# Mixture-of-experts stage: 32-row blocks on four column tiles instead of pairs of 64-row blocks, in a two-layer trunk

## The reference

```
def grouped_expert_mlp(h, expert_id, w_gate, w_up, w_down):
    '''Evaluate only the selected experts: assignments are sorted by expert into EXPERT_BLOCK-row
    segments (each padded to a block multiple) and every block is run through its own expert.
    h: (N, D); expert_id: (N, K) -> (N, K, D).'''
```

```
layer 0:  73 30 51 12 71 45 82 44 128 231 49 145 174 205 146 334 22 102 84 18 109 52 44 43 39 15 25 36 49 56 7 39
layer 1:  42 21 14 87 41 178 91 12 65 55 16 57 37 2 70 4 9 25 6 23 10 2 12 25 177 156 10 66 6 5 548 176
```

## Time and profile before

| | |
|---|---|
| median of 3 runs | 5775.29 us |
| profiled execution | 5788.05 us, of which span 5785.7 us |
| TensorE (PE) busy | 4182.2 us, 72% |
| VectorE (DVE) busy | 2196.7 us, 38% |
| ScalarE (ACT) busy | 1422.0 us, 25% |
| DMA moved | 778.83 MB, mean 135 GB/s |
| weights of the experts | 3 x 64 transfers of 2048 KB |

### The profile page before, as it was taken

How to read it: one execution, slowest core, us unless ns; L and a number is a source line. 1 busy time by engine, 2 the same in 40 slices (tenths; PEclk the granted TensorE clock), 3 DMA queues, 4 the chain that set the end, 5 groups by cost and what they waited for, 6 DMA issues and landing times. The chain is left out here.

```text
span 5785.7 us, 71070 instructions
## 1 busy us (share of the span) xinstructions
PE 4182.2 (72%) x23474; PEld 2739.1 (47%) x23475; DVE 2196.7 (38%) x4254; ACT 1422.0 (25%) x3188; POOL 639.3 (11%) x1135
## 2 busy tenths in 40 slices
PE   5597599395876949574499983598199955497893
PEld 1385377284765838453133321487056644132331
DVE  0312544666556656624000002411677733200003
ACT  0210254343333424212011110210056622011111
POOL 0000000131322313300100002000300010100001
PEclk9798799697988969786799996799599977799997
DMA  9421100101010010133886697322510023799943
GB/s 336 147 86 68 62 9 9 38 1 25 10 25 10 0 34 1 46 128 109 312 339 235 228 377 282 118 89 76 193 49 10 11 98 105 274 364 397 374 165 145
DMA packets 350063, 778.83 MB, mean 135 GB/s; under 512 B 52000, under 2 KB 95284, under 8 KB 349796
## 3 DMA queue, kind: packets, MB, share of 16 engines
q1 hardware_dynamic: 297640, 624.64, 30.1%
q10 hardware_dynamic: 37696, 103.04, 4.6%
q0 software_dynamic: 14544, 48.79, 2.4%
HBM read 656.45 MB, written 122.58 MB: 135 GB/s over the span
## 5 line engine op out<-in xcount | busy, mean ns | idle before, releaser
L2306 PE MATMUL ex_bG<-ex_w,ex_xT 128*64 x880 | 424.7, 639 | 134.5 <-SPq L2227 77.3
L2306 PE MATMUL ex_bY<-ex_w,ex_aT 128*64 x880 | 392.6, 599 | 74.5 <-DVE ex_aT L2369 59.7
L2309 PE MATMUL ex_bG<-ex_w,ex_xT 128*64 128x512 f32 x880 | 424.7, 639 | 0.0
L367 PE MATMUL p_acc<-hT,p_wh 128*128 128x512 f32 (+1 forms) x1056 | 376.2, 356 | 24.6 <-DVE p_wl L379 24.6
L2309 PE MATMUL ex_bY<-ex_w,ex_aT 128*64 128x512 f32 x880 | 392.8, 600 | 0.0
L2306 PE MATMUL ex_bU<-ex_w,ex_xT 128*64 x880 | 386.6, 592 | 0.0
L2309 PE MATMUL ex_bU<-ex_w,ex_xT 128*64 128x512 f32 x880 | 386.6, 592 | 0.0
L2367 DVE TENSOR_TENSOR ex_a<-ex_sg,ex_bU 128x512 f32<-128x512 f32 x55 | 37.9, 688 | 917.9 <-PE ex_bU L2309 917.9
L367 PE MATMUL p_acc<-hT_rest,p_wh 128*128 128x512 f32 (+1 forms) x1056 | 375.7, 356 | 0.0
L367 PE MATMUL p_acc<-hT,p_wl 128*128 128x512 f32 (+1 forms) x1056 | 375.2, 355 | 0.0
L2306 PEld LDWEIGHTS ex_bG<-ex_w,ex_xT 128*64 128x64 f32 x880 | 127.9, 148 | 415.3 <-issue 415.3
(11 more groups left out here) (362 smaller groups left out, 8841.4 us busy)
## 6 DMA issues: line engine op xcount, KB each, us to landing
ex_w<-in_moe_w_gate SPq DMA_DIRECT2D x64, 2048.0 KB, 17.8
ex_w<-in_moe_w_up SPq DMA_DIRECT2D x64, 2048.0 KB, 21.2
ex_w<-in_moe_w_down SPq DMA_DIRECT2D x64, 2048.0 KB, 18.1
mods_w<-in_mod_w SPq DMA_DIRECT2D x24, 2048.0 KB, 13.0
projT_dram<-p_o ACTq DMA_DIRECT2D x44, 640.0 KB, 2.9
yb_dram<-ex_y ACTq DMA_DIRECT2D x55, 512.0 KB, 6.3
p_w<-in_od_w_in SPq DMA_DIRECT2D x12, 1024.0 KB, 5.1
n_x<-x_dram SPq DMA_DIRECT2D x20, 512.0 KB, 4.1
```

Source lines behind the costliest of these rows:

```text
L367: mm = nc.tensor.matmul(acc[u % 2][c][:, 0:n], a[:, u // 2, k, at], b[:, k, t0:t0 + n], start=k == 0 and x == 0, stop=k == KT - 1 and x == 2)
L2306: nc.tensor.matmul(bank[0:BR, :], stationary[:, k, 0:BR], w[:, ds(slot0 + (offset + k * n), 512)], start=k == 0, stop=k == tiles - 1)
L2309: m = nc.tensor.matmul(bank[BR:P, :], stationary[:, k, BR:P], w[:, at:at + 512], start=k == 0, stop=k == tiles - 1)
```

## The change

The experts run in **blocks of 32 rows**, in their natural order, one block after the other (97 in layer 0, 85 in layer 1, since they run in fours and one more).

- Rows are gathered as 128 pieces of 256 values: piece c of row t lies on partition 32c + t. For this the norm phase writes each row's columns in a permuted order (`placed`), and the route phase makes four piece numbers from each token number.
- TensorE works on four column tiles of 32. In `hidden` two tiles compute gate (columns 0 to 255 and 256 to 511), two compute up, all from the same 32 rows, 32 products of 256 columns; in `down` each tile computes a quarter of the result, 16 products of 256 columns. Turning the rows and the hidden is done with products by the identity matrix, 8 of 128 columns and 8 of 64.
- In the loop, the hidden of block b is followed by the down of block b-1, the turn of the rows of block b+2 and the turn of the hidden of block b. The code of a block is read from `table` for `hidden` and again for `down`, and each time picks one of three arms.
- The result has four buffers of 32 x 1024 on 128 partitions (`y`), each stored with its own semaphore; the zero fill uses the same shape.
- Weights are fetched in longer contiguous pieces: each partition takes 16 KB of gate, 16 KB of up and 2 x 8 KB of down, where it took 2 KB and 4 KB pieces.
- ScalarE only applies Silu and starts the stores; all copies are VectorE's.

The diff, cut to its core (constants, the norm phase, the route phase's end and the experts phase):

```diff
+        if rows_out is None:
+            natural = placed = lambda z: z
+        else:
+            natural = lambda z: z.rearrange("p (m c e) -> p m c e", c=XG, e=2)
+            placed = lambda z: z.rearrange("p (c e m) -> p m c e", c=XG, e=2)
...
-                        nc.vector.tensor_tensor(h[:, u, :], h0[:, u, :], mod[:, cond, 0, :], ALU.add).then_inc(h_done, 1)
+                        nc.vector.tensor_tensor(placed(h[:, u, :]), natural(h0[:, u, :]), natural(mod[:, cond, 0, :]), ALU.add).then_inc(h_done, 1)
...
-BR = 64
-NPM = (2 * TOK + NE * (BR - 1)) // BR // 2 + 1
-NPT = NPM + 1
-NBT = 2 * NPT
+BR = 32
+CAP = TOK // BR
+NBM = (2 * TOK + NE * (BR - 1)) // BR
+NBT = NBM + 4
+MQ = (NBM + 2) // 4
 WR = 3
...
-                pe.wait_ge(back_in, 16)
-                nc.tensor.transpose(bankT[:, 0:NPT], back[:, :], ident[0:NPT, 0:NPT]).then_inc(back_t, 1)
+                pe.wait_ge(spread_done, 1)
+                nc.tensor.transpose(bankT[:, 0:NBT], back4[:, :, :].rearrange("n c t -> n (c t)"), ident[0:NBT, 0:NBT]).then_inc(back_t, 1)
...
+                dve.wait_ge(back_in, 16)
+                nc.vector.tensor_scalar(back4[:, :, :], back[:, :].rearrange("n (o t) -> n o t", o=1).to_broadcast([NBT, XG, BR]), float(XG), None, ALU.mult).then_inc(spread_done, 1)
                 dve.wait_ge(back_t, 1)
-                c.did(V.tensor_copy(tok[:, :], bankT[:, 0:NPT]))
+                c.did(V.tensor_scalar(tokf[:, :], bankT[:, 0:NBT], quad[:, 0:1], None, ALU.add))
+                c.did(V.tensor_copy(tok[:, :], tokf[:, :]))
...
-                        sp.wait_ge((g_done, u_done, y_done)[part], (1, 1, 2)[part] * tiles)
+                        sp.wait_ge((h_done, h_done, y_done)[part], tiles)
                     name, at, kk, n = (("moe_w_gate", 0, KT, EH), ("moe_w_up", UP, KT, EH), ("moe_w_down", DOWN, HT, D))[part]
-                    sp.dma_start(w[:, u * WCOLS + at:u * WCOLS + at + kk * n].rearrange("p (o k n) -> p o k n", o=1, n=n),
-                                 wv(name)[:, ds(e, 1), :, :]).then_inc(w_in[part][u], 16)
+                    to = w[:, u * WCOLS + at:u * WCOLS + at + kk * n]
+                    if part < 2:
+                        sp.dma_start(to.rearrange("p (o k n) -> p o k n", o=1, n=n),
+                                     d[name][layer].rearrange("e (p k) n -> p e k n", k=kk)[:, ds(e, 1), :, :]).then_inc(w_in[part][u], 16)
+                    else:
+                        sp.dma_start(to.rearrange("p (o g n) -> p o g n", o=1, g=2),
+                                     d[name][layer].rearrange("e (g p h) n -> p e g (h n)", g=2, h=2)[:, ds(e, 1), :, :]).then_inc(w_in[part][u], 16)
...
+                def hidden(p, u):
+                    for c in range(XG):
+                        for e in range(2):
+                            for g in range(4):
+                                at = u * WCOLS + (0, UP)[g // 2] + (2 * c + e) * EH + g % 2 * HC
+                                m = nc.tensor.matmul(bH[p][g * BR:(g + 1) * BR, 0:HC], xT[:, p, e, c, :], w[:, at:at + HC],
+                                                     start=c == 0 and e == 0, stop=c == XG - 1 and e == 1)
+                    m.then_inc(h_done, 1)
+
+                def down(p, u):
+                    for k in range(HT):
+                        for g in range(4):
+                            at = u * WCOLS + DOWN + k * D + g * XC
+                            m = nc.tensor.matmul(bY[p][g * BR:(g + 1) * BR, 0:XC], aT[:, p, k % 2, k // 2, :], w[:, at:at + XC], start=k == 0, stop=k == HT - 1)
+                    m.then_inc(y_done, 1)
+
+                def turn_hidden(p):
+
+                    for h in range(2):
+                        for g in range(4):
+                            t = nc.tensor.matmul(bA[p][g * BR:(g + 1) * BR, h * 2 * BR:(h + 1) * 2 * BR], a[:, p, h, g * BR:(g + 1) * BR], ident[:, 2 * BR:P], start=True, stop=True)
+                    t.then_inc(atr, 1)
...
                 with pe.Fori(0, n) as i:
+                    for q in PAR:
+                        b, p = 2 * i + q + 1, 1 - q
+                        need, slot = place(b)
+                        for part in range(2):
+                            pe.wait_ge(w_ready[part], need)
+                        pe.wait_ge(xT_done, b + 1)
                         for u in range(WR):
+                            with pe.If(slot == u):
+                                hidden(p, u)
+                        block_down(b - 1, 1 - p)
+                        turn_rows(p, i + q + 2, b)
+                        turn_hidden(p)
...
+                def store(b, p):
+                    act.wait_ge(ye_done, b + 1)
+                    act.dma_start(yb[ds(b * BR, BR), :].rearrange("t (c n) -> c t n", c=XG), y[:, p, :]).then_inc(y_out[p], 16)
...
+                def result(b, u, i):
+                    dve.wait_ge(y_done, b + 1)
+                    dve.wait_ge(y_out[u], 16 * i + 16)
+                    nc.vector.tensor_copy(y[:, u, :], bY[u % 2][:, 0:XC]).then_inc(ye_done, 1)
...
                 with dve.Fori(0, n) as i:
+                    for u in range(4):
+                        b, p = 4 * i + u + 1, (u + 1) % 2
+                        product(b, p)
+                        hidden_turned(b, p)
+                        rows_turned(b + 2, p)
+                        result(b - 1, u, i)
```

More of the change, by code:

```diff
@@ L2231, in step @@
                     e = load(sp, ds(o + T_EXP, 1), NE - 1)
-                    tiles = load(sp, ds(o + (T_PEND - WR), 1), NPM, 1) if free else None
+                    tiles = load(sp, ds(o + (T_PEND - WR), 1), NBM, 1) if free else None
                     for part in range(3):
@@ new lines, in place @@
+                def place(b):
+                    code = load(pe, ds(b + T_CODE, 1), WR * (NE + 1) - 1, WR)
+                    return code // WR, code % WR
+                def hidden(p, u):
+                    for c in range(XG):
+                        for e in range(2):
+                            for g in range(4):
[3 more added lines that the diff above has]
+                    m.then_inc(h_done, 1)
@@ new lines, in block_down @@
+                def block_down(b, p):
+                    need, slot = place(b)
+                    pe.wait_ge(w_ready[2], need)
+                    pe.wait_ge(aT_done, b + 1)
+                    for u in range(WR):
+                        with pe.If(slot == u):
+                            down(p, u)
+                turn_rows(0, 1)
+                turn_rows(1, 1)
+                pe.wait_ge(w_ready[0], 1)
+                pe.wait_ge(w_ready[1], 1)
+                pe.wait_ge(xT_done, 1)
@@ L2359, in _ @@
+                for u in range(4):
+                    act.sem_inc(y_out[u], 16)
+                gated(0, 0)
+                with act.Fori(0, n) as i:
+                    for u in range(4):
+                        gated(4 * i + u + 1, (u + 1) % 2)
+                        store(4 * i + u, u)
+                store(4 * n, 0)
+                for u in range(4):
+                    act.wait_ge(y_out[u], 16 * n + (16 if u else 32))
+                    act.sem_inc(ended, 1)
             @block.vector
@@ L2376, in combine_phase @@
+                product(0, 0)
+                hidden_turned(0, 0)
+                rows_turned(2, 0)
+                with dve.Fori(0, n) as i:
+                    for u in range(4):
+                        b, p = 4 * i + u + 1, (u + 1) % 2
[3 more added lines that the diff above has]
+                        result(b - 1, u, i)
+                result(4 * n, 0, n)
 def combine_phase(nc, sems, tag, d, layer, yb, src, dst, slots, gates, first=0, final_gain=None):
```

214 lines of the change are left out of this document (94 added, 120 removed).

## The result

The changed kernel takes 5954.19 us (median of 4; 5944.65 to 5962.9) against 5780.74 before: a ratio of 1.030 with an interval of 1.0278 to 1.0321. It is 3.0% slower. The experts' stages grew from 767 and 747 us to 855 and 820. That is 161 of the 165 us by which the span grew (5785.7 to 5950.4); the norm and route phases cost next to nothing.

The account below looks back on a forecast made before the run. Each expert was taken as bound by the larger of TensorE's blocks and its weights, 1502 us in sum; 1706 with period 8.1 and floor 17.5, plus 10 for stalls, gave +214: 5985 us, range 5750 to 6090.

Parts of the forecast that it names:

- The sign: Whole kernel: slower than before, chance 0.78, from sequencer work between groups and result stores on four DMA engines.
- the period: TensorE's loop in the experts' stages: 8.1 us per 32-row block, from 5.8 of products and 2.3 of gaps.
- the floor of a weights' set: Weight fetches per expert: about 17.5 us on the engines that also carry stores, 15.9 without stores.
- the stalls: Result buffers in the experts' stages: a full set holds VectorE, then TensorE; 10 us added, bounds 0 and 150.
- The stream of products: TensorE per 32-row block: 3.43 us gate and up, 1.72 down, 0.64 turns; 5.79 in sum.
- The sequencer's term: TensorE's place code per block: uncovered gaps of 0.65 us before down, 1.4 before hidden, 0.2 loop end; 2.3 in all.
- the lead of 20 records: TensorE's sequencer runs some 20 records ahead, covering 1.07 us before down and 0.32 before hidden.
- the sum of maxima: Experts' stages: each expert costs the larger of its blocks' time and its weights' time; 1502 us before, 1706 forecast.
- A single cause: Rivals for the whole kernel: only the sequencer, 5890 us, chance 0.13; only the stores, 5830 us, chance 0.12.
- The faster case: Rival: sequencer's lead covers the place code and stores spread over the engines; -142 us, 5635; chance 0.17.
- The column tiles: Rival on TensorE: column tiles run two at a time, not four; period 12.9 us, time 6665; chance 0.04.
- The clock: Rival on TensorE: short gaps lower the granted clock to 0.86; +60 to +100 us, 6070; chance 0.06.

Follow-up runs that it names:

- the kernel with both edits: Changed kernel with the block table read once per block behind the down products, and results stored by four transfers over sixteen engines: 5746.15 us, ratio 0.9928.
- 5739: The kernel with both edits, with TensorE's wait for the gate product moved from ahead of the rows' turn to ahead of the hidden's: 5739.1 us.

## Why the prediction was right

**The sign and its two causes were right; that the number came so close is in part luck.** I forecast 5985 with 5750 to 6090, and 0.78 for slower; it is 5954. Both steps that made it slower were shown apart: the sequencer's work ahead of gate and up (+123 with a read more, -89 with a read less, nothing from VectorE's copy) and the stores on four engines (-95 with sixteen, +206 with two). But three terms of the sum were off. Two were too large (the period and the floor of a weights' set) and one too small (the stalls), and they nearly cancelled.

**The stream of products** was nearly right: 64 and 32 records at the pace of four tiles side by side. Where a block follows without a gap the period is 6.0 us with the turns (3218.91 to 3224.93 with fewer table reads), where I had 5.79.

**The sequencer's term was a third too large.** I took gaps of 2.3 us per block for a period of 8.1; the period is 7.7, so 1.7 over the 6.0. Ahead of gate and up I forecast 1.4, and 1.8 in every second block with the loop's end; it is 0.94 to 1.66. Ahead of down I forecast 0.65, and there is at most 0.29. The step that was off is the lead of 20 records, read from the long products of before. In the changed kernel the read for down starts at 3224.5 while gate and up run until 3225.87: 1.4 us ahead, some 26 records, which covers nearly all of the sequencer's work. The Trainium skill ("TensorE: Matmul & The Clock Gate") gives a depth of 64 for this queue; 26 records with their loads are 52 entries, nearer to it than my 40, so the page came closer for this gap; no gap ahead of down would have followed from it, and almost none is there. The gap ahead of gate and up stayed.

**The floor of a weights' set was too high.** I put 17.5 us: 15.9 without stores and 1.5 for a store on four engines. Measured are 16.3 to 16.7 us with four-engine stores and 15.5 with spread ones. The 15.9 came from the short pieces of before, and I gave the longer pieces 0 to -20 us and then nothing; they are worth some 55. Four engines in place of sixteen add 0.8 to 1.2 us to the set, where I had 1.6.

**The stalls were too small, and sit elsewhere than I wrote.** I gave them 10 us. With the measured 7.7 and a floor of 16.6 the sum of maxima is 1620, +118 to 1502; the stages grew by 161, so some 43 us are left for stalls and for the lower clock behind them. I forecast that full buffers hold VectorE; that is 42 us in 26 waits. The larger part is ScalarE, held in the issue of the transfer for up to 11.65 us, with the Silu behind it. I had named what is queued behind VectorE's wait, but not what is queued behind the issuing instruction. That an issue can take so long stood in the trace of the kernel before, for weights on SP's queue (shortest/median/longest in ns; layer 0's stage):

```profile
L2221 SPq DMA_DIRECT2D ex_w<-in_moe_w_up x32: 372/4632/9285, 2778.0 to 3494.9; - x32
```

The time of a store beside the weights was right (22 us under gate and up and 12 under down forecast, 21 and 11 by the measured turns). What I did not draw from it is that only one store per expert then gets through while 25 of the 32 experts of layer 0 and 15 of layer 1 have two blocks or more.

**The sum of maxima itself** holds within 20 us where neither cost is left: with a period of 6.6 us (17 gate products from 3192.2 to 3298.0 in the kernel with both edits) and a floor of 15.5 it gives 1441, 61 less than before, and that kernel is 43 faster than before.

**The rivals.** A single cause was excluded by the two runs that each take one away. The faster case (neither cost) is the kernel with both edits: it is faster, but by 0.7% and not by the 142 us that I gave it, since its period is 6.2 to 7.1 and not 5.8. The column tiles do run four at a time. The clock is no cause of the gaps of the sequencer: from 3200 to 3300 it is 1.00 in both kernels, with TensorE busy for 82%. It does add to the stalls, as the 6.57 us above show; how much in all no run separates.

What stays open: the last 7 us between 5739 and 5746, and how the 43 us divide between the stalls and the clock.

## What to carry to other kernels

Smaller blocks shrink the work that hides the sequencer: what is read, computed and branched on per block must be set against the time of the queued products ahead of it, and read where that queue is longest. Here the outermost count of a transfer decided how many DMA engines carry it, and a store on few engines suffers most beside queues with long pieces; four transfers of 32 rows beat one of 4 x 32. To see whether such a store keeps up, count pieces and not bytes: pieces of the store per engine against pieces that the other queue has for that engine in the same time. The issue that then blocks holds all that its engine has to do next. And a releaser in a profile is the last event before a gap ends: delaying it costs one run and tells whether it is the cause.

## What the runs showed of the hardware

- The issue of a transfer can block its engine: with 4-engine stores beside 16 KB pieces 34 of 182 issues took over 1 us, up to 11.65, for a usual 0.555; with two engines up to 23.4; with sixteen at most 1.8, in the kernel with both edits.
- An engine takes pieces in turn by queue whatever their length: one 1 KB piece of a store in 0.67 us beside pieces of 16 KB, in 0.35 beside 8 KB, in 0.13 beside 2 KB. The same stores had no issue above 1.2 us beside pieces of 2 and 4 KB.
- Long pieces move weights faster: 5746 us with pieces of 16 and 8 KB against 5802 with 2 and 4 KB (and twice the transfers), for 403 MB of weights.
- After a stall of 17 us the granted clock was 0.54 (from 5457 to 5463), and the same 64 records took 6.57 us in place of 3.66.
- A loop body with twice the code cost 1008 us; code packets rose from 114 to 640.
